# Mixture-of-experts rows packed in blocks of 32: twelve tiles of four column groups in place of sixteen tiles of one expert, with packed weights

## What is computed

```
combine = jnp.sum(jax.nn.one_hot(idx, N_EXPERTS, dtype=jnp.float32) * w[..., None], axis=-2).astype(x.dtype)
y = jnp.zeros_like(x)
for e in range(N_EXPERTS):
    h = jax.nn.silu(x @ w_gate[e]) * (x @ w_up[e])
    y = y + (h @ w_down[e]).astype(x.dtype) * combine[..., e:e + 1]
```

## Time and profile before

| | before |
|---|---|
| median of the runs | 1356.27 us |
| the profiled execution | 1357.32 us |
| its span | 1355.5 us |
| mean granted TensorE clock | 0.955 |
| PE busy | 1217.7 us (90% of the span) |
| PE weight loads | 693.4 us (51%) |
| DVE busy | 607.8 us (45%) |
| ACT busy | 266.5 us (20%) |
| POOL busy | 220.0 us (16%) |
| moved by DMA | 216.78 MB, mean 160 GB/s |

### The profile page before, as it was taken

One profiled execution on the slowest core, in us unless ns is written; L12 is line 12 of the kernel. 1 busy time (PEld: TensorE's weight loads), 2 busy tenths in 40 slices (PEclk: granted clock), 3 DMA queues, 4 the chain that ended last, 5 costly groups with the idle time before them and its releaser, 6 DMA issues.

```text
span 1355.5 us, 13771 instructions
## 1 busy us (share of the span) xinstructions
PE 1217.7 (90%) x4743; PEld 693.4 (51%) x4743; DVE 607.8 (45%) x1432; ACT 266.5 (20%) x630; POOL 220.0 (16%) x385
## 2 busy tenths in 40 slices
PE   8999999999999579999849799999999939999966
PEld 4447777545744244444325455775764424444422
DVE  2178888313723546433355130530443355643316
ACT  1204434122300001111102213332320001111110
POOL 0105445202001120000063200000001111000013
PEclk9999999998999789999969899999999969999978
DMA  8113012325361659999652410000115177999733
GB/s 333 62 63 140 1 68 102 119 90 34 51 217 57 211 171 372 345 368 370 251 187 72 169 62 0 1 0 1 63 42 206 43 241 267 360 362 367 266 140 120
DMA packets 108452, 216.78 MB, mean 160 GB/s; under 512 B 5053, under 2 KB 72157, under 8 KB 107233
## 3 DMA queue, kind: packets, MB, share of 16 engines
q1 hardware_dynamic: 90544, 153.35, 32.0%
q0 software_dynamic: 17552, 61.76, 14.5%
q10 hardware_dynamic: 288, 0.80, 0.2%
HBM read 181.02 MB, written 34.85 MB: 159 GB/s over the span
## 4 chain that ended last, share of the span: by engine, by line
PE 81%; DVE 9%; issue 3%; DMA 3%; ACT 2%; POOL 1%; SPq 0%; DVEq 0%; POOLq 0%; ACTq 0%
PE pair L1374 16%; PE pair L1283 10%; PE pair L1020 10%; PE pair L1393 8%; PE pair L1031 5%; PE pair L1203 5%; PE pair L1137 4%; PE pair L1467 3%; PE pair L1240 3%; PE pair L1516 2%; PE pair L1362 2%; PE pair L1238 1%; PE pair L1497 1%; PE pair L1061 1%; PE pair L1221 1%
## 5 line engine op out<-in xcount | busy, mean ns | idle before, releaser
L1020 PE MATMUL pair<-ring,xT 128*128 128x512 f32 (+1 forms) x320 | 138.9, 593 | 0.7 <-DMA ring<-in_even_w_in 0.7
L1374 PE MATMUL pair<-ring,arena 128*128 128x512 f32 x256 | 117.1, 612 | 3.5 <-DVE arena L2173 3.5
L1374 PE MATMUL pair<-arena 128*128 128x512 f32 x256 | 112.5, 592 | 0.0
L1020 PEld LDWEIGHTS pair<-ring,xT 128*128 128x128 f32 (+1 forms) x320 | 57.7, 182 | 76.4 <-issue 75.1
L1137 PE MATMUL pair<-xT,ring 128*128 128x296 f32 x320 | 83.4, 415 | 6.1 <-ACT arena L1552 3.0
L806 POOL TENSOR_SCALAR small<-small 128x1 f32<-128x1 f32 (+3 forms) x45 | 15.8, 352 | 433.7 <-DVE small L2054 390.4
L1374 PEld LDWEIGHTS pair<-ring,arena 128*128 128x128 f32 x256 | 50.0, 197 | 66.5 <-issue 66.5
L2193 DVE COPY arena<-pair 128x256 f32<-128x256 f32 x32 | 13.6, 423 | 156.2 <-PE pair L1382 156.2
L828 POOL TENSOR_TENSOR arena<-arena 128x128 f32<-128x128 f32 x140 | 56.6, 437 | 156.9 <-PE pair L1063 86.4
L1203 PE MATMUL pair<-arena 128*128 128x264 f32 (+5 forms) x280 | 79.1, 412 | 2.2 <-issue 1.4
L1374 PEld LDWEIGHTS pair<-arena 128*128 128x128 f32 x256 | 48.6, 190 | 61.2 <-issue 61.2
(11 more groups left out here) (354 smaller groups left out, 1879.2 us busy)
## 6 DMA issues: line engine op xcount, KB each, us to landing
arena<-in_moe_w_gate SPq DMA_DIRECT2D x16, 1024.0 KB, 7.2
arena<-in_moe_w_up SPq DMA_DIRECT2D x16, 1024.0 KB, 9.8
arena<-in_moe_w_down SPq DMA_DIRECT2D x16, 1024.0 KB, 11.5
ring<-in_moe_w_gate SPq DMA_DIRECT2D x16, 1024.0 KB, 7.9
ring<-in_moe_w_up SPq DMA_DIRECT2D x16, 1024.0 KB, 10.2
ring<-in_moe_w_down SPq DMA_DIRECT2D x16, 1024.0 KB, 12.2
y_rows<-arena SPq DMA_DIRECT2D x32, 512.0 KB, 9.7
ring<-in_even_w_in SPq DMA_DIRECT2D x5, 2048.0 KB, 7.4
```

Of the source, the lines that this page charges most:

```text
L1020: last = pe.matmul(ps[0:P, 0:n], xT[:, k, 128 * i:128 * i + P], w[:, k, :], start=(k == 0), stop=(k == chunks - 1))
L1374: last = pe.matmul(bank, xgT[:, e % 2, k, :], gu[:, k, :], start=(k == 0), stop=(k == KD - 1))
```

## The change

**Slots.** Every expert now owns 96 slots, three blocks of 32 (`CAPS`, `BASE`), laid end to end over 12 tiles. A tile has four blocks; `BLOCKS[x]` names the expert of each. Four experts fill three tiles: 0 0 0 1, then 1 1 2 2, then 2 3 3 3, and so on. What is over 96 goes to overflow tiles, of which up to 12 are allowed (9 before), and as many are zeroed early in the program. With the counts above, expert 2 of layer 1 (97 rows) is over by one row, and no other.

**Matmuls.** Each matmul of `gate_up` and `down` becomes four with 32 stationary columns, one for each block, into the block's own 32 partitions of PSUM and with the moving weights of its own expert. The transposes and the work of ACT and DVE on a tile stay as they are. An overflow tile is computed as before.

**Weights.** Gate and up are packed on the host into one array and all weights are laid out as the chip reads them, 16 KB and 8 KB in a row for each partition. An expert is two DMAs, 2 MB and 1 MB. `LAST[e]` is the last tile that uses expert e: 0, 1, 2, 2, 3, 4, 5, 5, 6, 7, 8, 8, 9, 10, 11, 11. SP loads the gate and up of expert e + 4 after `gate_up(LAST[e])` and its down matrix after `down(LAST[e])`. `gate_up(x)` waits for both loads of each expert in the tile.

**One-hots** are cut where a tile changes expert: ten narrower instructions a tile in place of five. Groups of two tiles are six in place of eight.

```diff
-NOV = 9
-NSLOTS = (NE + NOV) * 128
+CAPS = [96] * 16
+BASE = [sum(CAPS[:e]) for e in range(NE)]
+NX = sum(CAPS) // 128
+NOV = 12
+NSLOTS = (NX + NOV) * 128
+BLOCKS = [[next(e for e in range(NE) if BASE[e] <= 128 * x + 32 * j < BASE[e] + CAPS[e]) for j in range(4)]
+          for x in range(NX)]
+LAST = [max(x for x in range(NX) if e in BLOCKS[x]) for e in range(NE)]
...
-        IX_GROUPS = [range(e, e + 2) for e in range(0, NE, 2)]
+        IX_GROUPS = [range(x, min(x + 2, NX)) for x in range(0, NX, 2)]
         LAST_IX = len(IX_GROUPS) - 1
...
+            def load_gate_up(l, e):
+                sp.dma_start(expert_place(e)[0], gu_d[l * NE + e]).then_inc(we_in[e % 4].sem, 16)
+
+            def load_down(l, e):
+                sp.dma_start(expert_place(e)[1], down_d[l * NE + e]).then_inc(we_in[e % 4].sem, 16)
+
             def load_expert(l, e):
-                gu, dn = expert_place(e)
-                s = we_in[e % 4].sem
-                sp.dma_start(gu[:, :, 0:DE], gate_d[l * NE + e]).then_inc(s, 16)
-                sp.dma_start(gu[:, :, DE:2 * DE], up_d[l * NE + e]).then_inc(s, 16)
-                sp.dma_start(dn, down_d[l * NE + e]).then_inc(s, 16)
+                load_gate_up(l, e)
+                load_down(l, e)
 
...
-                for e in range(NE):
-                    if e + 4 < NE:
-                        sp.wait_ge(*dn_ps[(l, e)])
-                        load_expert(l, e + 4)
-                    sp.wait_ge(*y_sa[(l, e)])
-                    sp.wait_ge(*y_sd[(l, e)])
-                    sp.dma_start(y_rows[l][128 * e:128 * e + 128, :], yb[:, e % 2, :]).then_inc(y_st[e % 2].sem, 16)
-                    if l == 0 and e == 13:
-                        for n in range(n_items0, n_items0 + 4):
+                for x in range(NX):
+                    freed = [e + 4 for e in range(NE - 4) if LAST[e] == x]
+                    sp.wait_ge(*gu_ps[(l, x)])
+                    for e in freed:
+                        load_gate_up(l, e)
+                    sp.wait_ge(*dn_ps[(l, x)])
+                    for e in freed:
+                        load_down(l, e)
+                    sp.wait_ge(*y_sa[(l, x)])
+                    sp.wait_ge(*y_sd[(l, x)])
+                    sp.dma_start(y_rows[l][128 * x:128 * x + 128, :], yb[:, x % 2, :]).then_inc(y_st[x % 2].sem, 16)
+                    if l == 0 and x == LAST[12]:
+                        load_item(n_items0)
...
-                        sp.dma_start(gu[:, :, 0:DE], gate_d[bass.ds(le, 1)].rearrange("o p k n -> p (o k) n")
-                                     ).then_inc(mk["w"], 16)
-                        sp.dma_start(gu[:, :, DE:2 * DE], up_d[bass.ds(le, 1)].rearrange("o p k n -> p (o k) n")
+                        sp.dma_start(gu, gu_d[bass.ds(le, 1)].rearrange("o p k n -> p (o k) n")
                                      ).then_inc(mk["w"], 16)
                         sp.dma_start(dn, down_d[bass.ds(le, 1)].rearrange("o p k n -> p (o k) n")
                                      ).then_inc(mk["w"], 16)
...
+                for x in (NX - 2, NX - 1):
+                    pool.wait_ge(*y_st[x % 2][(l, x)])
                 for i in range(3):
                     gather_rows(l, i)
...
             def gate_up(l, e):
-                pe.wait_ge(*we_in[e % 4][(l, e)])
+                for x in sorted(set(BLOCKS[e])):
+                    pe.wait_ge(*we_in[x % 4][(l, x)])
                 pe.wait_ge(*xgT_sa[(l, e)])
                 pe.wait_ge(*xgT_sd[(l, e)])
                 if e >= 2:
                     pe.wait_ge(*h_sb[(l, e - 2)])
-                gu, _ = expert_place(e)
                 bank = psum[1][:, 512 * (e % 2):512 * (e % 2) + 512]
                 for k in range(KD):
-                    last = pe.matmul(bank, xgT[:, e % 2, k, :], gu[:, k, :], start=(k == 0), stop=(k == KD - 1))
+                    for j, x in enumerate(BLOCKS[e]):
+                        c = slice(32 * j, 32 * j + 32)
+                        last = pe.matmul(bank[c, :], xgT[:, e % 2, k, c], expert_place(x)[0][:, k, :],
+                                         start=(k == 0), stop=(k == KD - 1))
                 last.then_inc(gu_ps.sem, 1)
...
                     for k in range(2):
-                        last = pe.matmul(psum[2][:, 512 * half:512 * half + 512], hT[:, e % 2, 128 * k:128 * k + 128],
-                                         dn[:, k, 512 * half:512 * half + 512], start=(k == 0), stop=(k == 1))
+                        for j, x in enumerate(BLOCKS[e]):
+                            c = 32 * j
+                            last = pe.matmul(psum[2][c:c + 32, 512 * half:512 * half + 512],
+                                             hT[:, e % 2, 128 * k + c:128 * k + c + 32],
+                                             expert_place(x)[1][:, k, 512 * half:512 * half + 512],
+                                             start=(k == 0), stop=(k == 1))
                 last.then_inc(dn_ps.sem, 1)
 
             def experts(l):
                 rows_t(l, 0)
-                for e in range(NE + 1):
-                    if e < NE:
+                for e in range(NX + 1):
...
-                for m in (256.0, 384.0, 512.0):
+                chain(tt(cnt, cnt, const("caps"), ALU.subtract))
+                chain(ts(ovn, cnt, 0.0, None, ALU.is_gt))
+                for m in (128.0, 256.0, 384.0):
                     chain(stt(ovn, cnt, m, ovn, ALU.is_gt, ALU.add))
                 chain(dve.tensor_tensor_scan(ovend, const("ones")[:, 0:NE], ovn, 0.0, ALU.mult, ALU.add))
                 copy(ovi[:, 0:1], ovend[:, NE - 1:NE])
                 chain(tt(cnt, ovend, ovn, ALU.subtract))
-                chain(ts(cnt, cnt, 128.0, float(NE * 128 - 128), ALU.mult, ALU.add))
+                chain(ts(cnt, cnt, 128.0, float(NX * 128), ALU.mult, ALU.add))
+                chain(tt(cnt, cnt, const("caps"), ALU.subtract))
                 chain(tt(ovn, const("base"), cnt, ALU.subtract))
-                chain(ts(R[6], R[5], 128.0, None, ALU.is_lt))
...
-                for e in IX_GROUPS[g]:
+                for x in IX_GROUPS[g]:
                     for i in range(NT):
-                        last = ts(oneh[:, e % 2, i, :], iotab[:, :], 1.0, rk1[:, i, e:e + 1], ALU.add, ALU.is_equal)
+                        for e in sorted(set(BLOCKS[x])):
+                            lo = 32 * BLOCKS[x].index(e)
+                            hi = lo + 32 * BLOCKS[x].count(e)
+                            last = ts(oneh[:, x % 2, i, lo:hi], iotab[:, lo:hi], float(128 * x - BASE[e] + 1),
+                                      rk1[:, i, e:e + 1], ALU.add, ALU.is_equal)
                     last.then_inc(oh_sb.sem, 1)
...
+    tiles_of = lambda w: np.asarray(w).reshape(2 * NE, -1, 128, w.shape[3]).transpose(0, 2, 1, 3)
+    inputs = {**inputs, "moe_w_down": tiles_of(inputs["moe_w_down"]),
+              "moe_w_gate_up": tiles_of(np.concatenate([inputs["moe_w_gate"], inputs["moe_w_up"]], 3))}
```

More of the change, by code:

```diff
@@ L940, in experts @@
                     pool.wait_ge(*x_st[b][last])
-                for e in range(NE):
+                for e in range(NX):
                     for g in range(len(IX_GROUPS)):
```

80 lines of the change are left out of this document (40 added, 40 removed).

## The result

The changed kernel takes **1439.9 us** (median of 4, 1434.1 to 1443.4) against 1356.7 of the kernel before: 83 us slower. The ratio on record, with its 95% interval, is 1.0595 [1.0565, 1.0624]; the two medians alone give 1.061. 1401 was forecast, with 1432 as the upper end. The sign was right, the size was not, and the range missed.

The account below looks back on a forecast made before the run. PE was taken to set the experts' pace, DMA engines close behind. Terms -91.2 + 4.8 + 66 + 24 + 38 + 1.8 + 1.7 = +45.1 on 1357.3 gave 1402.4, or 1401 us at the median; range 1358 to 1432.

Parts of the forecast that it names:

- start of the stage of layer 0: First gather of a layer waits for twenty narrower one-hots in place of ten: 2 x 0.9 = +1.8 us.
- The late down matrix: PE waits for a down matrix before gate_up at tiles 3, 4, 6, 7, 9, 10: twelve at 5.5 us, +66 us.
- Rival 2: Expert stage: DMA queue full, down matrices land in 7.2 us or more; 1421 us, or 1430 with slower clock; chance 0.14.
- The overflow tile: After layer 1's twelve tiles, one overflow tile for expert 2 runs in series: +38 us, between 30 and 48.
- Wrong if under 30: Overflow term fails if layer 1's last store to first gather of results takes under 30 us.
- the end of 48: Overflow tile's upper end, 48 us: down at low clock too, and 5 us for loop code that never ran before.
- The clock: gate_up behind each of twelve waits runs slower at lower granted clock: 2.0 us each, +24 us.
- The groups: gate_up and down in four column groups: 0.1 us per entry, two a turn, 24 turns, +4.8 us.
- rival 3: In gate_up and down, groups don't run four at once for long: 1425 us, chance 0.05.
- The last store: End of layer 0: three mixer weights issued one tile before the last delay the last store, +1.7 us, between 0 and 5.
- Rival 1: Waits at gate_up of tiles 3, 4, 6, 7, 9, 10 stay short, 3.0 us each: 1335 us, chance 0.13.
- Rival 4: Layer 1: no overflow tile runs, as ranks on the chip differ by one row: 1363 us, chance 0.05.

Follow-up runs that it names:

- the last kernel: The 1313.6 kernel with POOL's residual and norm-weight loads behind each layer's last gather and two mixer weights behind layer 0's last store: 1292.9 us.
- the floor: Changed kernel with only the first four experts of each layer loaded, later ones using weights in place: 1339.8 us, layer 0's stage 148.9 us.
- the fillings: Changed kernel with matmuls nobody reads ahead of the six waiting gate_ups of a layer: 1441.9 us with 40, 1425.8 us with 20.
- the own semaphores: Changed kernel with separate semaphores for down matrices; gate_up waits for gate and up alone, down for its own matrix: 1377.2 us.
- the 128 slots: Changed kernel with 128 slots for expert 2 and 64 for expert 11, so no row overflows: 1388.8 us.
- 1313.6: Changed kernel with own down-matrix semaphores, 128 slots for expert 2, and gate and up loads issued before SP's wait for down and store: 1313.6 us.

## Why the prediction was wrong in size and right in sign

By the profiled executions, 1441.3 us of span against 1355.5. The first row of the table was not measured by itself: it is the forecast's own figure, and the second takes up what the stages leave over.

| term | forecast | found |
|---|---|---|
| eight turns less | -91.2 | -91.2 |
| column groups | +4.8 | +6.7, with about -4 of small effects in the stages: +2.6 |
| twelve waits for a down matrix | +66 | +83.8 |
| clock behind them | +24 | +27.5 |
| overflow tile | +38 | +48.8 |
| start of the stage of layer 0 | +1.8 | +2.3 |
| end of layer 0 | +1.7 | +6.8 |
| end of layer 1 beside the overflow tile | 0 | +3.4 |
| between the two layers' experts | 0 | +1.8 |
| sum | +45.1 | +85.8 |

*The late down matrix* was the right mechanism at the right six tiles, mis-sized by 18 us: 5.5 us a wait were taken, 7.0 found. The step that failed is the sentence that what is ahead in SP's queue was "issued about 18 us earlier, which is time enough". At tiles 3, 6 and 9 it was 7.5, 10.2 and 10.5 us, because the store of the tile before stands between the load and the `gate_up` that frees its place. These six waits averaged 8.5 us, 18 us over six of 5.5. The undisturbed case was right: 4.95 us against "5.1 us alone". The forecast also named the 2 MB behind a down matrix without a price for them; how the 3 us on top of 5.5 share out between the load ahead and the 4 MB behind isn't shown, and the long wait of tile 4 (6.94 and 5.81 us) stays open. Rival 2, "the queue is full", is nearer, with 7.2 us a wait and 1421 to 1430 us. Its limit from 368 GB/s is not: 51 us were to be left without any waits, and the last kernel runs its two stages 6 and 3 us over the floor. Nor was 368 GB/s a ceiling, as the stretch of 416 shows.

*The overflow tile* was short by 11 us. Of these 3.6 are the step "the longer of the gather with its transposes and the weights": they share the engines, so the gather lands in 10.5 us and transposes and copy come after it. The turns of the loop take 6.1 us and not 3.6 (the chain from 1384.7 to 1390.77); `down` runs at low clock, 5.9 us and not 3.7, which the forecast had as an end of its range. The other 2.5 lie in the steps between. "Wrong if under 30" did not come to pass, but the end of 48 did not hold it either.

*The clock* was right: 2.3 us a wait against 2.0, and the fillings show that it is its own cost. *The groups* cost 0.28 us a turn against 0.2, and rival 3 is out. The Trainium skill (TensorE: Matmul & The Clock Gate, Part 3) gives 2.38 times for three column tiles; here the 32 matmuls of a `gate_up` in four groups take 7.05 us and the eight at full width 7.03, and a whole turn is 2.5% longer. *The last store* of layer 0 was taken at 1.7 us and the end of the layer grew by 6.8; with the mixer weights behind it 4 of these went. *Rival 1* did not come, and its threshold of 3.7 us for a wait with its clock was too high. In the trace of the own semaphores 21.3 us of waits and 8.4 us of clock come to 2.5 us for each of the twelve, and that execution is still 9 us slower than before. By the table, a wait with its clock would have had to cost under 2.1 us: the overflow tile and the ends of the layers had been priced too low there too. *Rival 4* has the mechanism that the 128 slots show; it did not happen by itself. Larger packets were given nothing, and got nothing.

The range failed since four terms, the wait, the overflow tile, the clock and the ends of the layers, came out above what was taken for them, while each had been given its bounds by itself. For the six waits, the gather of the overflow tile and the last store of layer 0 the reason is the same: each was put near the price of a transfer that has the engines to itself. Of the table's small rows, the -4 among the groups is mostly two things. In the turn of tile 4 the kernel before waited 1.3 and 1.1 us for DVE, which the weights now hide (that turn took 13.2 and 13.0 us, its neighbours 11.7); and of `slot_tokens` there are two groups fewer in each layer, at 0.3 us each. The 3.4 and 1.8 us are not broken down.

## What to carry to other kernels

When loads are tied more closely to their use, price a transfer by what its queue holds at that moment, in the order in which the issuing engine can really get to it, waits included. Give each part of a tile's weights its own semaphore before shortening its distance. Bulk loads that nobody needs soon belong behind the last small gather of their queue: their place alone was worth 33 us here against tile 8, and some 17 against tile 3, where they had stood (1313.6 to 1292.9, less the 4 of the mixer weights).

## What the runs showed of the hardware

A gather of 128 rows landed in 4.3 us with the engines free, in 10.5 beside 3 MB of weights, and in 36.9 behind 3.4 MB of its own queue and beside the weights of another (issued at 558.57, used at 595.52). Filling a wait with idle matmuls kept the granted clock at 1.00 in a stretch that had 0.50 without, and made the next 64 matmul records 2.6 us shorter. In the changed kernel a down matrix of 1 MB landed in 4.8 us at tiles 7 and 10 and in 5.7 and 6.8 at tile 4, with nothing left ahead of it in its queue, and in 7.3 to 9.1 us with 2 MB ahead of it still under way. Cutting the packets from 108452 to 42403 changed nothing, with the loads off PE's chain.
